# Expert weights of a top-4-of-32 mixture of experts: experts taken one by one, in 32 KB runs, with slots refilled by quarters at both ends of the pass

## The reference, cut to what matters

```
gu   = xb @ w_gate_up[e] + b_gate_up[e]          # xb: rows of the tokens of expert e; w_gate_up[e] is 1024 x 2048
x_glu = min(gu[:, :1024], 7);  x_lin = clip(gu[:, 1024:], -7, 7)
act  = x_glu * sigmoid(1.702 * x_glu) * (x_lin + 1)
yb   = act @ w_down[e] + b_down[e]               # w_down[e] is 1024 x 1024
out[tokens of e] += gate * yb
```

## Time and profile before

| | us |
|---|---|
| time before, median of 3 runs | 1188.18 (1186.94 to 1188.24) |
| the profiled execution, its own time | 1186.9 |
| its span, first to last instruction | 1184.9 |
| PE busy | 1122.8 (95%) |
| chain that ended last | PE 68%, DMA 23%, DVE 6% |
| bytes read from HBM | 432.13 MB |

### The profile page before, as it was taken

The page is one execution under the profiler, slowest core; times in us unless marked ns, Lnnn a source line. Parts: engine busy times, 40 slices in busy tenths (PEclk is TensorE's granted clock), DMA queues, the critical chain, the costliest instruction groups (busy, mean ns, idle before and its releaser), DMA issues.

```text
span 1184.9 us, 13680 instructions
## 1 busy us (share of the span) xinstructions
PE 1122.8 (95%) x5446; PEld 527.0 (44%) x5446; DVE 292.7 (25%) x727; ACT 215.3 (18%) x354; POOL 14.2 (1%) x27
## 2 busy tenths in 40 slices
PE   8999999999999999999999999999999999999996
PEld 6878888554343434343434333333333343333332
DVE  2256442132121221212212121212121212121212
ACT  2437781021001010100111011001100110111011
POOL 3010000000000000000000000000000000000000
PEclk9999999999999999999999999999999999999998
DMA  9813237659999999999999999999999999999994
GB/s 313 263 37 117 98 108 294 247 214 425 395 425 430 425 428 426 429 426 428 428 427 427 428 426 428 426 429 426 428 426 428 426 428 426 427 428 426 429 426 163
DMA packets 53360, 433.52 MB, mean 366 GB/s; under 512 B 4650, under 2 KB 21192, under 8 KB 24632
## 3 DMA queue, kind: packets, MB, share of 16 engines
q1 hardware_dynamic: 52112, 429.98, 87.7%
q0 software_dynamic: 960, 2.30, 0.6%
q10 hardware_dynamic: 264, 0.93, 0.2%
HBM read 432.13 MB, written 1.05 MB: 366 GB/s over the span
## 4 chain that ended last, share of the span: by engine, by line
PE 68%; DMA 23%; DVE 6%; issue 1%; SPq 0%; DVEq 0%; ACT 0%
PE psum L1568 21%; PE psum L1600 20%; DMA ring<-in_w_gate_up 11%; DMA arena<-in_w_gate_up 11%; PE psum L1408 4%; PE psum L1458 3%; PE psum L1611 2%; PE psum L1208 2%; PE psum L1387 2%; PE psum L1427 2%; PE psum L1544 2%; DVE arena L1079 2%; PE psum L1168 1%; PE psum L1581 1%; DVE arena L1088 1%
## 5 line engine op out<-in xcount | busy, mean ns | idle before, releaser
L1568 PE MATMUL psum<-ring,arena 128*64 128x512 f32 x1024 | 229.7, 596 | 7.1 <-DMA ring<-in_w_gate_up 6.6
L1568 PE MATMUL psum<-arena 128*64 128x512 f32 x1024 | 229.7, 596 | 7.0 <-DMA arena<-in_w_gate_up 6.9
L1079 DVE TENSOR_TENSOR arena<-psum,biasT 128x512 f32<-128x512 f32 x64 | 44.0, 688 | 424.3 <-PE psum L1544 424.3
L1568 PEld LDWEIGHTS psum<-ring,arena 128*64 128x64 f32 x1024 | 70.6, 137 | 152.7 <-issue 141.5
L1568 PEld LDWEIGHTS psum<-arena 128*64 128x64 f32 x1024 | 69.7, 137 | 153.0 <-issue 134.3
L1600 PE MATMUL psum<-arena 128*64 128x512 f32 x512 | 118.4, 623 | 17.3 <-DVE arena L1090 17.3
L1600 PE MATMUL psum<-ring,arena 128*64 128x512 f32 x512 | 118.4, 623 | 16.7 <-DVE arena L1090 16.7
L962 DVE TENSOR_TENSOR h<-h,psum 128x1024 f32<-128x1024 f32 x32 | 39.1, 1222 | 258.3 <-PE psum L1611 258.3
L699 ACT ACTIVATE arena<-psum 128x1024 f32<-128x1024 f32 x32 | 32.8, 1024 | 341.8 <-PE psum L1568 341.8
L1600 PEld LDWEIGHTS psum<-arena 128*64 128x64 f32 x512 | 39.0, 143 | 91.2 <-issue 91.2
L1600 PEld LDWEIGHTS psum<-ring,arena 128*64 128x64 f32 x512 | 37.7, 143 | 91.9 <-issue 73.7
(11 more groups left out here) (225 smaller groups left out, 780.4 us busy)
## 6 DMA issues: line engine op xcount, KB each, us to landing
arena<-in_w_gate_up SPq DMA_DIRECT2D x64, 2048.0 KB, 27.7
ring<-in_w_gate_up SPq DMA_DIRECT2D x64, 2048.0 KB, 27.9
arena<-in_w_down SPq DMA_DIRECT2D x16, 2048.0 KB, 28.4
arena<-in_w_down SPq DMA_DIRECT2D x32, 1024.0 KB, 28.9
ring<-in_w_down SPq DMA_DIRECT2D x16, 2048.0 KB, 30.0
ring<-in_w_down SPq DMA_DIRECT2D x32, 1024.0 KB, 29.6
ring<-in_w_in SPq DMA_DIRECT2D x14, 1024.0 KB, 12.0
ring<-in_w_out SPq DMA_DIRECT2D x4, 1024.0 KB, 4.9
```

Source lines behind the costliest of these rows:

```text
L1079: return v.tensor_tensor(dst.rearrange("p (m j) -> p m j", m=8), src, bias[:, m:m + 8, bass.ds(pair + e, 1)].broadcast_to([P, 8, CAP]), AL ...
L1568: ins = mm(bank[2 + 2 * e + n][h * CAP:(h + 1) * CAP, :], xg[:, c, e * CAP:(e + 1) * CAP], eslot(base + k)[:, (2 * j + h) * D + n * 512:(2 ...
```

## The change

**Slots and runs.** `GU_ROWS` is 4 and `DN_ROWS` is 8: four slots of 4 MB in place of eight of 2 MB, and one partition's run in HBM is 32 KB (8192 elements). Three slots make one expert: two of gate and up, one with all its down rows. The separate loads of the last down rows are gone.

**Order of experts.** PE works on single experts, each one step ahead: gate and up of expert x+1, then down of expert x, then its scatter. Gate and up of expert 0 stand before the loop. `features` of expert x stand in the middle of gate and up of expert x+1, for every expert. The wait for an activation stands before `down(x)`.

**Refill.** The first eight slot loads behind the prefetch (`first_refill`) are issued in quarters of 1 MB, each when its quarter has been read; `used` now counts quarters. The loop's loads are whole slots. The last four slots (`last_loads`) come as one whole and then in quarters with a semaphore each, and PE waits for quarters. Half of the last expert's down rows, 2 MB, is loaded before the loop into `kept`, between the loads of slot 2 and slot 3, and is multiplied ahead of the other half.

**Down and scatter.** The two halves of the array's columns now hold the two halves of one expert's output row (`bank[1][n * CAP:(n + 1) * CAP]`), and one ACT copy takes both out. The scatter is done for each expert: four products contracted over 64 rows, n = 0 from rows 0 to 63 and n = 1 from rows 64 to 127 of `pickgT` and `yr`. It was four products over 128 rows for a pair.

**Biases.** The four bias products in each pair and the DVE copy for them are gone. Once, after three turns of two pairs, gate weights times down biases are computed for all tokens and added.

**DVE and the end.** Adds of scattered rows stand once for each expert. Before the loop DVE reads the pass count back ahead of `gathered`. At the end DVE multiplies tile 1 with the gain while ACT sums squares, and DVE and ACT each scale one tile; ACT stores tile 1.

```diff
-GU_ROWS = 2
+GU_ROWS = 4
...
+EXPERT_LOADS = GU_LOADS + 1
+QUARTERS = 4
+REFILL_END = 3 * ESLOT
+BIAS_TURN = 3
...
+            def first_refill(base):
+                for idx in range(ESLOT, REFILL_END):
+                    for q in range(QUARTERS):
+                        sp.wait_ge(wide_used[idx % ESLOT], base + QUARTERS * (idx // ESLOT - 1) + q + 1)
+                        quarter_of(idx, rows_of(idx - GU_LOADS, 1), q,
...
+            sp.wait_ge(s_mg, 4)
+            sp.dma_start(kept, down_rows(EXPERTS - 1)[:, EWIDTH // 2:EWIDTH]).then_inc(s_kept, 16)
...
-            gathered(0)
...
             with dve.Fori(0, n_pass) as b:
...
+                gathered(b * PAIRS)
...
+            def expert_pair(tb, u):
...
+                gate_up(tb, o, 1, 2, None, first_features)
+                pick_rows(x, 0)
+                down(tb, o + 2, x)
+                scatter(x)
+                pe.wait_ge(s_pick, g + 1)
+                gather(0)
+                gather(1)
+                gate_up(tb, o + 3, 0, 2, g * 2 + 2, second_features)
+                for t in range(2):
+                    pe.wait_ge(s_acc[t], x + 1)
+                pick_rows(x + 1, 1)
+                down(tb, o + 5, x + 1)
+                scatter(x + 1)
...
+            def scatter(x):
+                pe.wait_ge(s_pgt, x + 1)
+                pe.wait_ge(s_y, x + 1)
                 for t in range(2):
                     for n in range(2):
-                        pe.wait_ge(s_y, g * 2 + (n + 1))
-                        ins = mm(bank[4 + 2 * t + n], pickgT[:, t * P:(t + 1) * P],
-                                 yr[:, n * 512:(n + 1) * 512], start=True, stop=True)
+                        ins = mm(bank[4 + 2 * t + n], pickgT[n * CAP:(n + 1) * CAP, t * P:(t + 1) * P],
+                                 yr[n * CAP:(n + 1) * CAP, :], start=True, stop=True)
                     ins.then_inc(s_sc, 1)
...
-            with pe.Fori(0, n_pass) as b:
-                with pe.Fori(0, TURNS) as j:
```

641 lines of the change are left out of this document (408 added, 233 removed).

## The result

The changed kernel takes **1177.45 us** (median of 4 executions, 1173.46 to 1179.0) where the kernel before, on the same chip, takes 1187.56 us (4 executions, 1186.59 to 1188.24). The ratio is 0.991, with a 95% interval of 0.988 to 0.994. A later set gave 1175.6 us for the changed kernel and a ratio of 0.989 (0.988 to 0.991). The forecast was 1177.

What follows compares the result with a forecast made beforehand. The saturated DMA stream of weights bounds the kernel; bytes loaded ahead -4.9, start -1.2, gap -2.6, longer runs -3.5, PE 0 and tail +1 sum to -11.2 us, giving 1177 us (bounds of the terms 1170 to 1184; range 1168 to 1189).

## What to carry to other kernels

Bytes taken out of a saturated stream are worth their time only ahead of the last transfer that somebody waits for. Find the last wait that a load ends, and take the bytes from before it; the same buffer gave 0 us at the end and 4 to 5 us at the start. Price a longer run from two sizes of packet in the trace (a fixed cost for each and a slope), never from a stretch of a few packets. When a tail is worked out from a transfer, use the time at which it is complete and not its share of the bytes, ask whether anybody waits for it, and write each edit's gain and its loss in the tail side by side. Before two profiles are subtracted, look whether the clock fell in both for as long.

## What the runs showed of the hardware

A packet cost 12.4 ns on top of 301 ns for each 8 KB, at all of 8, 16 and 32 KB, so that the stream stands at 421.8, 428.2 and 431.6 GB/s (packets of 4 KB took 159 ns, 4 less than that line gives), and an endless run would give an estimated 435 (16 engines x 8192 B / 301 ns). Loads of 64 partitions, with the same runs and all 16 engines busy, ran at 212 GB/s. Two products on different 64-row halves overlap (0.25 us each against 0.47). The granted clock fell to half at the router in 12 of 14 profiles, for 10.2 us (in seven, from 243.1 to 245.3 us on) or 3.4 us (in five, from 247.6 to 250.0 us on), in executions in which PE's work was the same up to there. Such a spell costs only where PE is on the chain: 3.1 us before the first refill (10.2 us long), 1.7 and 2.9 us after a last wait (3.4 and 6.8 us long). The spells behind earlier waits, as at 974.8 and 1032.8 us, leave no mark: the waits for down rows end 58.2 to 58.4 us apart either way.
